# The last attention with V as the stationary operand, and its gate z kept by features

## The chip, the cores and the metric

The kernel runs on one core of one Trainium2 chip, as one program. The metric is the device time of an execution in microseconds. A profile is one further execution, taken by the hardware profiler. The engines have one instruction stream each and meet only at semaphores: TensorE (PE; its weight loads are listed as PEld), VectorE (DVE), ScalarE (ACT), GpSimd (POOL, all but unused here) and SyncE, which issues the loads.

## The reference, cut to what matters

Two transformer stacks follow each other on 256 tokens of width 1024. The change is in the last mixer of the second stack, a latent attention with 16 heads. Names are those of the kernel.

```python
xn = rmsnorm(x, g)                       # (256, 1024)
c, k_rope, z = xn @ w_in                 # latents 384 + 256, one rotary key, z (256, 1024)
q, kv = rms(c_q) @ w_qb, rms(c_kv) @ w_kvb   # 16 heads: 64 plain + 32 rotary features, V of 64
s = q_h @ k_h.T / sqrt(96)               # per head 256 x 256
p = softmax(s)                           # along the keys
o = (p @ v_h) * silu(z_h)                # per head 256 x 64
y = concat(o) @ w_out                    # (256, 1024)
```

After it come the residual, a norm, a gated projection and the final norm.

## The kernel before

All activations stay on the chip; weights stream through a ring of three slots, in units of at most 2048 columns. Each unit u is loaded to `raw`; ACT copies it to `high` (L582, a rounded value) and DVE subtracts to get `low` (L980); PE then multiplies three products per tile: high by high, high by low, low by high (`mm3`, L1565). The helper `behind(u)` on ACT and on DVE does this preparation for unit u + 3, so the place of each `behind` call in an engine's stream decides what stands in front of what. Nothing is scheduled by a planner: the order of each engine is the order of the code.

The projection z (PE L2067, `z_unit`) is made by tokens: the activations are stationary, 512 columns of weights move. Its result lies tokens by features in four banks; ACT takes it with a Silu scaled per token by `rcol` (L886). `rcol` is the inverse root of the norm, turned into a column by two PE transpositions (`root_columns(2)`, L1899) and a small DVE copy (`columns(2)`, L1329). Meanwhile DVE makes the norms of the latents: it reads the sums of squares that `latent_sums` (L2057) put into bank 2, takes a root (`newton`), scales five latents (L1505), and splits them for the next products.

The score products of heads 0 to 3 are put between the last units of the projections (j = 6 in the loop at L2101). The attention then runs over the 16 heads (PE L1955, ACT L789, DVE L1394). For each head PE transposes the exponentials `E2` in four pieces (`transposed`), ACT copies them to `PT2` (L797), and PE multiplies with the turned probabilities stationary and 65 columns of V moving, the 65th a column of ones, so that it gives the sum. DVE inverts the sum (L1401) and multiplies result, inverse and z (L1404). Scores of a pair of heads (two row tiles of 64, L2095 and L2097) are put in two pairs ahead. DVE takes the row maximum (L1392), ACT the exponential (L785). After the last head PE transposes the 16 pieces of the result back to features (`output_group`, L1980), ACT and DVE split them, and the output projection `feature_out` (L1863) begins.

The order of DVE around the start of the attention is: `behind` of the kvb units, the maxima of heads 0 to 3, `behind(first["mla_kvb"] + 3)` (L1527), and then `attention(False)`. ACT's is: exponentials of heads 0 and 1 at j = 6, the copies of j = 7, `behind` of the last kvb unit, and then the copy of the first turned head.

## Time and profile before

| | |
|---|---|
| median of 3 runs | 1094.41 us (1092.81 to 1095.01) |
| the profiled execution | 1093.67 us |
| its span, first to last instruction | 1091.9 us |
| granted clock, mean | 0.988 |
| PE / PEld busy | 95% / 88% of the span |
| DVE / ACT busy | 72% / 46% |
| DMA, mean | 192 GB/s |

PE's matmuls overlap in the profile, since each record also holds the time in the pipe: the step from one start to the next is what an instruction costs. A product of two plain float32 operands makes two records, a transposition one, and one of the three products of `mm3` one.

### The profile page before, as it was taken

Reading aid. Unit: us, or ns where it says so; the run is one execution under the profiler, and the core shown is the slowest. Engines: PE = TensorE matmul, PEld = TensorE weight load, DVE = VectorE, ACT = ScalarE, POOL = GpSimd, SP = SyncE. Lnnn points to the kernel's source line nnn. Section 1 sums busy time; section 2 is a strip of 40 time slices with the busy share of each in tenths; the row PEclk is TensorE's granted clock in tenths of the full one; section 3 lists DMA queues with packets and bytes.
Section 4 is the critical chain, followed back from the end, with each engine's and each line's share of the span. In section 5 each row is a group of like instructions: output and inputs, shape, how many; then the busy total and the mean of one; then the engine's idle time right before and its main releaser. Section 6 shows DMA issues by size and latency. Waiting matters only on the chain. (4 is left out here: it accounts for less than half of the span.)

```text
span 1091.9 us, 18245 instructions
## 1 busy us (share of the span) xinstructions
PE 1038.2 (95%) x7726; PEld 965.1 (88%) x7726; DVE 784.3 (72%) x1177; ACT 507.2 (46%) x700; POOL 0.7 (0%) x6
## 2 busy tenths in 40 slices
PE   4899999799999999998999999999999999999995
PEld 2689875699999999998999999999987998888984
DVE  3689759668788787887985656568736569786565
ACT  3623238554434334324443434445347556547462
POOL 0000000000000000000000000000000000000000
PEclk9899999999999999999999999999999999999998
DMA  9769541038898987566646666554754053445020
GB/s 368 269 210 337 185 173 39 2 117 292 307 317 291 312 289 237 196 222 228 242 165 221 201 234 219 176 175 149 234 183 139 7 192 127 162 166 198 1 78 38
DMA packets 116545, 210.15 MB, mean 192 GB/s; under 512 B 4251, under 2 KB 78193, under 8 KB 116465
## 3 DMA queue, kind: packets, MB, share of 16 engines
q1 hardware_dynamic: 115716, 206.81, 55.1%
q10 hardware_dynamic: 748, 2.18, 0.5%
q8 instruction: 61, 1.00, 0.4%
q14 instruction: 20, 0.16, 0.0%
HBM read 207.92 MB, written 1.05 MB: 191 GB/s over the span
## 5 line engine op out<-in xcount | busy, mean ns | idle before, releaser
L980 DVE TENSOR_TENSOR low<-raw,high 128x2048 fp32r<-128x2048 f32 (+2 forms) x147 | 328.1, 2234 | 159.8 <-ACT high L582 159.4
L582 ACT ACTIVATE high<-raw 128x2048 fp32r<-128x2048 f32 (+2 forms) x147 | 272.9, 1866 | 215.2 <-PE PS L1569 113.3
L1652 PE MATMUL PS<-hH,high 128*128 128x258 f32 x896 | 221.9, 284 | 4.5 <-ACT high L582 1.9
L1653 PE MATMUL PS<-hL,high 128*128 128x258 f32 x896 | 220.3, 283 | 0.0
L1652 PEld LDWEIGHTS PS<-hH,high 128*128 128x128 f32 x896 | 169.8, 189 | 6.4 <-issue 2.8
L1653 PEld LDWEIGHTS PS<-hL,high 128*128 128x128 f32 x896 | 168.7, 188 | 0.1
L1671 PE MATMUL PS<-hH,low 128*128 128x258 f32 x896 | 126.2, 283 | 0.3
L1671 PEld LDWEIGHTS PS<-hH,low 128*128 128x128 f32 x896 | 115.6, 189 | 1.4 <-DVE low L980 1.4
L1567 PE MATMUL PS<-gH,high 128*128 128x256 f32 x352 | 98.4, 280 | 0.0
L1568 PE MATMUL PS<-gL,high 128*128 128x256 f32 x352 | 98.4, 280 | 0.0
L1569 PE MATMUL PS<-gH,low 128*128 128x256 f32 x352 | 98.2, 279 | 0.0
L959 DVE SCALAR_TENSOR_TENSOR ada_acc<-ada_raw,cond,ada_acc 128x1024 f32<-128x1024 f32 x70 | 89.7, 1281 | 4.9 <-DMA ada_raw<-in_ada_w 2.7
L1567 PE MATMUL PS<-oH,high 128*128 128x256 f32 x256 | 73.9, 289 | 2.4 <-issue 1.8
L1568 PE MATMUL PS<-oL,high 128*128 128x256 f32 x256 | 73.3, 286 | 0.0
L1569 PE MATMUL PS<-oH,low 128*128 128x256 f32 x256 | 73.1, 286 | 0.0
L723 ACT ACTIVATE sil<-ta,shifts 128x256 f32<-128x256 f32 x44 | 20.0, 502 | 110.8 <-DVE ta L1224 110.8
L1567 PEld LDWEIGHTS PS<-gH,high 128*128 128x128 f32 x352 | 66.2, 188 | 0.2 <-DVE gL L1251 0.2
L1568 PEld LDWEIGHTS PS<-gL,high 128*128 128x128 f32 x352 | 66.0, 187 | 0.0
L1569 PEld LDWEIGHTS PS<-gH,low 128*128 128x128 f32 x352 | 66.0, 187 | 0.0
L1567 PEld LDWEIGHTS PS<-oH,high 128*128 128x128 f32 x256 | 49.5, 193 | 2.9 <-issue 1.8
L1567 PE MATMUL PS<-high,hH 128*128 128x512 f32 x128 | 51.3, 401 | 0.8 <-DVE low L980 0.8
L1568 PE MATMUL PS<-low,hH 128*128 128x512 f32 x128 | 50.4, 394 | 0.0
(315 smaller groups left out, 1935.3 us busy)
## 6 DMA issues: line engine op xcount, KB each, us to landing
raw<-in_ffn_w_in SPq DMA_DIRECT2D x44, 1024.0 KB, 6.2
ada_raw<-in_ada_w SPq DMA_DIRECT2D x82, 512.0 KB, 5.4
raw<-in_ffn_w_out SPq DMA_DIRECT2D x22, 1024.0 KB, 6.2
raw<-in_na_w_in SPq DMA_DIRECT2D x16, 1024.0 KB, 5.5
raw<-in_da_wqkv SPq DMA_DIRECT2D x12, 1024.0 KB, 8.7
raw<-in_sc_w_in SPq DMA_DIRECT2D x12, 1024.0 KB, 6.3
raw<-in_ple_w_gate SPq DMA_DIRECT2D x8, 1024.0 KB, 4.8
raw<-in_mla_w_in SPq DMA_DIRECT2D x7, 1024.0 KB, 5.3
```

Source lines behind the costliest of these rows:

```text
L582: nc.scalar.activation(high[s][:, 0:width(u)], raw[s][:, 0:width(u)], ACT.Copy).then_inc(high_ready, 1)
L723: ins = nc.scalar.activation(sil[:, c, :], ta[:, c, :], ACT.Silu, bias=shifts[:, c:c + 1])
L959: V_.scalar_tensor_tensor(acc[:, :], ada_raw[p % RING][:, :], cond[:, k, 0:1], acc[:, :], ALU.mult, ALU.add).then_inc(ada_used_dve, 1)
L980: V_.tensor_tensor(low[s][:, 0:w], raw[s][:, 0:w], high[s][:, 0:w].bitcast(F), ALU.subtract).then_inc(low_dve, 1)
L1567: MM(o, wH, xH, start=start, stop=False, skip_group_check=shared)
L1568: MM(o, wH, xL, start=False, stop=False, skip_group_check=shared)
L1569: return MM(o, wL, xH, start=False, stop=stop, skip_group_check=shared)
L1652: MM(PS[:, b + c, 0:SEQ + 2], high[s][w(j, c)], hH[:, j, 0:SEQ + 2], start=j == 0, stop=False)
L1653: MM(PS[:, b + c, 0:SEQ + 2], high[s][w(j, c)], hL[:, j, 0:SEQ + 2], start=False, stop=False)
L1671: last = MM(PS[:, b + c, 0:SEQ + 2], low[s][w(j, c)], hH[:, j, 0:SEQ + 2], start=False, stop=j == KC - 1)
```

## The change

It has four parts. First, the units of z are 256 columns wide over the whole depth, and PE makes z by features (`shared_features`: weights stationary, 256 tokens moving), one bank per unit; the banks are 3, 1, 2, 3. DVE scales each bank by the root, ACT takes the Silu in place on `zT` (the memory of X). The transposition of the root and its copy are gone. Secondly, the exponential of this attention also gives its row sums (`accum_out`), and DVE makes for each head two diagonal matrices with the inverses of the sums. PE turns E2 by a plain float32 product with such a diagonal instead of a transposition. Thirdly, V is stationary, 64 columns of it, and the 256 columns of the turned probabilities move; two heads lie side by side in partitions 0 to 63 and 64 to 127 of one bank. Fourthly, the results come out by features: DVE multiplies four heads at a time by z, ACT and DVE split them, and the 16 transpositions at the end are gone. The output projection waits for one quarter of them per unit.

```diff
-Z_BANK = ((3, 1), (2, 3))
+Z_BANK = (3, 1, 2, 3)
...
-    for c0 in (768, 768 + 512):
-        for half in range(2):
-            cols("mla", w["mla_w_in_2"][0], 4 * half, 4, c0, 512, 2)
+    for j in range(4):
+        cols("mla", w["mla_w_in_2"][0], 0, KC, 768 + 256 * j, 256, 1)
...
+        zT = X[:, :, :].rearrange(by_feature, n=SEQ)
+        diagonal = XN[:, 0, :].rearrange("p (i n) -> p i n", n=P)
...
-                                               bias=nmax[:, 2 * h + t:2 * h + t + 1])
+                                               bias=nmax[:, 2 * h + t:2 * h + t + 1],
+                                               accum_out=None if biased else esum[:, 2 * h + t:2 * h + t + 1])
...
-            act.wait_ge(root_column, 2)
-            for nb in range(2):
-                ua = first["mla_z"] + 2 * nb
...
-                for t in range(TT):
-                    act.wait_ge(blocks_done, blocks_before(ua + 1) + t + 1)
-                    nc.scalar.activation(Zg[:, t, 512 * nb:512 * nb + 512], bank(Z_BANK[nb][t]), ACT.Silu, scale=rcol[:, t:t + 1]).then_inc(vz_copied, 1)
...
+            for j in range(4):
+                behind(first["mla_z"] + j)
+                if j == 2:
                     for f0, f1 in ((0, 3), (3, 5)):
                         act.wait_ge(latent_staged, f1)
                         high_of(aH[:, f0:f1, :], latent[:, f0:f1, :])
+            for j in range(4):
+                act.wait_ge(z_scaled, j + 1)
+                nc.scalar.activation(zT[:, 2 * j:2 * j + 2, :], zT[:, 2 * j:2 * j + 2, :], ACT.Silu).then_inc(z_ready, 1)
...
-            attention(False)
...
+            def turned(h):
+                seen.next(made_a)
+                nc.scalar.activation(PT2[h % 2][:, :, :], bank(TURN_BANK[h % 2]).rearrange("p (k n) -> p k n", k=2), ACT.Copy).then_inc(probs_copied, 1)
+
+            def gated_high(q):
+                act.wait_ge(head_gated, 16 + q + 1)
+                high_of(oH[:, 2 * q:2 * q + 2, :], zT[:, 2 * q:2 * q + 2, :])
+
+            exps(2, False)
+            exps(3, False)
+            for p in range(8):
+                turned(2 * p)
+                turned(2 * p + 1)
+                if p + 2 < 8:
+                    exps(2 * p + 4, False)
+                    exps(2 * p + 5, False)
+                if p % 2 == 0 and p:
+                    gated_high(p // 2 - 1)
+            gated_high(3)
...
-            columns(2)
...
+            def z_bank(j):
+                v.wait_ge(blocks_done, block_end[first["mla_z"] + j])
+                V_.tensor_tensor(zT[:, 2 * j:2 * j + 2, :], bank(Z_BANK[j]).rearrange("p (k n) -> p k n", k=2), spread(rstd), ALU.mult).then_inc(z_scaled, 1)
+
             behind(first["mla_z"])
+            z_bank(0)
...
-            for u in range(first["mla_z"] + 1, first["mla_qb"]):
-                behind(u)
+            for j in range(1, 4):
+                behind(first["mla_z"] + j)
+                z_bank(j)
...
-            attention(False)
+
+            def diagonals(h):
+                seen.next(exp_ready)
+                link(V_.reciprocal(rsum[:, 2 * h:2 * h + 2], esum[:, 2 * h:2 * h + 2]))
+                for t in range(TT):
+                    ins = V_.tensor_scalar(diagonal[:, h % 4 * 2 + t, :], ident[:, :], rsum[:, 2 * h + t:2 * h + t + 1], None, ALU.mult)
+                ins.then_inc(diagonal_made, 1)
+
+            def gate_heads(q):
+                seen.next(value_made, 2)
+                z = zT[:, 2 * q:2 * q + 2, :]
+                V_.tensor_tensor(z, bank(VALUE_BANK[q % 2]).rearrange("p (k n) -> p k n", k=2), z, ALU.mult).then_inc(head_gated, 1)
+
+            def gated_low(q):
+                seen.next(split_high)
+                sl = slice(2 * q, 2 * q + 2)
+                V_.tensor_tensor(oL[:, sl, :], zT[:, sl, :], oH[:, sl, :].bitcast(F), ALU.subtract).then_inc(split_low, 1)
+
+            seen.n[exp_ready.name] = 32
+            v.wait_ge(z_ready, 4)
+            diagonals(0)
+            diagonals(1)
+            for p in range(8):
+                if p + 1 < 8:
+                    diagonals(2 * p + 2)
+                    diagonals(2 * p + 3)
+                if p + 2 < 8:
+                    scores(2 * p + 4, False)
+                    scores(2 * p + 5, False)
+                if p % 2:
+                    gate_heads(p // 2)
+                elif p:
+                    gated_low(p // 2 - 1)
+            gated_low(3)
...
-            z_unit(0, 0)
-            root_columns(2)
+            def z_unit(j):
+                shared_features(first["mla_z"] + j, Z_BANK[j])
+                owed(z_scaled, Z_BANK[j])
+
+            z_unit(0)
+            seen.n[root_ready.name] = 2
             latent_sums(2)
-            z_unit(0, 1)
-            z_unit(1, 0)
-            z_unit(1, 1)
+            for j in range(1, 4):
+                z_unit(j)
             seen.next(split_low, 2)
...
-            attention(mla_score, exp_ready)
-
-            outputs_around(None)
+            def turned_pair(p):
+                for h in (2 * p, 2 * p + 1):
+                    pe.wait_ge(diagonal_made, h + 1)
+                    b = TURN_BANK[h % 2]
+                    claim(b)
+                    for t in range(TT):
+                        for c in range(2):
+                            last = MM(PS[:, b, c * SEQ + t * P:c * SEQ + (t + 1) * P], E2[:, h % 4, t, c * P:(c + 1) * P],
+                                      diagonal[:, h % 4 * 2 + t, :], start=True, stop=True)
+                    last.then_inc(made_a, 1)
+                    owed(probs_copied, b)
+
+            turned_pair(0)
+            for p in range(8):
+                if p + 2 < 8:
+                    score_pair(2 * p + 4, mla_score, exp_ready)
+                seen.next(probs_copied, 2)
+                b = VALUE_BANK[p // 2 % 2]
+                if p % 2 == 0:
+                    claim(b)
+                for c in range(2):
+                    for e in range(2):
+                        last = MM(PS[64 * e:64 * e + 64, b, p % 2 * SEQ:(p % 2 + 1) * SEQ], V2[:, c, 2 * p + e, 0:64], PT2[e][:, c, :],
+                                  start=c == 0, stop=c == 1, tile_position=(0, 64 * e))
+                last.then_inc(value_made, 1)
+                if p % 2:
+                    owed(head_gated, b)
+                if p + 1 < 8:
+                    turned_pair(p + 1)
...
-            feature_out(first["mla_out"], (2, 0, 2, 0))
+            feature_out(first["mla_out"], (1, 1, 1, 1))
```

DVE at the start of the last attention: before, behind the subtraction for the last unit that is prepared there (`low`), come a maximum and the first head's inverse, which waits for a finished value product.

```order
L1392 TENSOR_REDUCE nmax<-PS 128x2 [waits score_made]
L1392 TENSOR_REDUCE nmax<-PS 128x2
L980 TENSOR_TENSOR low<-raw,high 128x2048 [waits high_ready]
L1392 TENSOR_REDUCE nmax<-PS 128x2 [waits score_made]
L1401 RECIPROCAL rsum<-PS 128x2 [waits value_made]
L1404 SCALAR_TENSOR_TENSOR XN<-PS,rsum,X 128x64 [waits dve_step]
L1404 SCALAR_TENSOR_TENSOR XN<-PS,rsum,X 128x64
```

```order
L1408 TENSOR_REDUCE nmax<-PS 128x2 [waits score_made]
L1408 TENSOR_REDUCE nmax<-PS 128x2
L996 TENSOR_TENSOR low<-raw,high 128x2048 [waits high_ready]
L1553 RECIPROCAL rsum<-esum 128x2 [waits exp_ready,z_ready]
L1555 TENSOR_SCALAR XN<-ident,rsum 128x128 [waits dve_step]
L1555 TENSOR_SCALAR XN<-ident,rsum 128x128
```

Now the diagonals (`XN<-ident,rsum`) stand behind the same subtraction, and what PE does first in the attention uses them.

PE in the last attention, a pair of heads in the middle: scores, then transpositions (L1578) and value products (L1975) head by head.

```order
L2095 MATMUL PS<-ml_kT,ml_qT 128x256 [waits exp_ready]
L2095 MATMUL PS<-ml_kT,ml_qT 128x256
L2097 MATMUL PS<-ml_krT,ml_qrT 128x256 x2
L2095 MATMUL PS<-ml_kT,ml_qT 128x256 x2
L2097 MATMUL PS<-ml_krT,ml_qrT 128x256 x2
L1578 MATMUL PS<-ident,E 128x128 [waits probs_copied,exp_ready]
L1578 MATMUL PS<-ident,E 128x128 x3
L1975 MATMUL PS<-V,PT 128x65 [waits head_gated,probs_copied]
L1975 MATMUL PS<-V,PT 128x65 x3
L1578 MATMUL PS<-ident,E 128x128 [waits probs_copied,exp_ready]
L1578 MATMUL PS<-ident,E 128x128 x3
```

```order
L2192 MATMUL PS<-XN,E 128x128 [waits diagonal_made,vz_copied,heads_copied,rope_part]
L2192 MATMUL PS<-XN,E 128x128 x3
L2192 MATMUL PS<-XN,E 128x128 [waits vz_copied,diagonal_made]
L2192 MATMUL PS<-XN,E 128x128 x3
L2141 MATMUL PS<-ml_kT,ml_qT 128x256 [waits exp_ready]
L2141 MATMUL PS<-ml_kT,ml_qT 128x256
L2143 MATMUL PS<-ml_krT,ml_qrT 128x256 x2
L2141 MATMUL PS<-ml_kT,ml_qT 128x256 x2
L2143 MATMUL PS<-ml_krT,ml_qrT 128x256 x2
L2207 MATMUL PS<-PT,V 64x256 [waits heads_copied,probs_copied]
L2207 MATMUL PS<-PT,V 64x256 x3
```

The second piece is the start of the attention in the changed kernel: both heads of a pair are turned together (L2192), then come the scores of a later pair, and four value products (L2207) do for two heads. The same kinds of rows repeat for each pair, without scores in the last two.

PE between the third and the fourth unit of z: the last products of the third unit and the first of the fourth, in the changed kernel.

```order
L1750 MATMUL PS<-hH,low 128x256 [waits low_dve]
L1750 MATMUL PS<-hH,low 128x256 x15
L1745 MATMUL PS<-hH,high 128x256 [waits z_scaled,high_ready]
L1746 MATMUL PS<-hL,high 128x256
```

Before, at the same place (third and fourth unit), with three rows that repeat for each tile:

```order
L1567 MATMUL PS<-high,hH 128x512
L1568 MATMUL PS<-low,hH 128x512
L1569 MATMUL PS<-high,hL 128x512
L1567 MATMUL PS<-high,hH 128x512 [waits low_dve]
L1568 MATMUL PS<-low,hH 128x512
```

The fourth unit waited only for its weights; now it takes bank 3 again, which DVE has to empty first (`z_scaled`).

## Rows read from the trace of the kernel before

**Rows 1.** Busy time by engine in 1000 to 1030 us (columns: stretch, engines, PEclk, DMA, GB/s).

```profile
1000.00:1030.00 30.00, 30.00 (x264) 27.21 (x263) 17.45 (x60) 17.54 (x41) 0.00 (x0) 1.00 0.10 36
```

**Rows 2.** Timeline of PE, last attention, one pair of heads (start, duration, instruction).

```profile
1010.21 0.70 PE L2095 MATMUL PS<-ml_kT,ml_qT 64*128 64x256 f32 x4
...
1012.14 0.66 PE L1578 MATMUL PS<-ident,E 128*128 128x128 f32 x4
1012.63 1.00 PE L1975 MATMUL PS<-V,PT 128*128 128x65 f32 x8
1013.47 0.61 PE L1578 MATMUL PS<-ident,E 128*128 128x128 f32 x4
...
1014.85 0.70 PE L2095 MATMUL PS<-ml_kT,ml_qT 64*128 64x256 f32 x4
```

**Rows 3.** Timeline of PE, first attention: a 128-column fp32 product beside a transposition.

```profile
200.50 1.16 PE L1858 MATMUL PS<-da_V,gates 128*128 128x128 f32 x8 [0.69 <-ACT gates L681]
201.49 0.60 PE L1578 MATMUL PS<-ident,gates 128*128 128x128 f32 x4
```

**Rows 4.** Timeline of PE, opening: four 32-column tiles in one PSUM bank.

```profile
19.73 0.62 PE L1753 MATMUL PS<-da_kT,cond 128*32 128x512 f32 x2 [0.41 <-DMA first_w<-in_ada_w]
19.74 0.62 PE L1753 MATMUL PS<-first_w,cond 128*32 128x512 f32 x2
20.18 0.60 PE L1753 MATMUL PS<-da_kT,cond 128*32 128x512 f32 x2
```

**Rows 5.** Timeline of PE, first and last waits of the last attention.

```profile
995.74 0.63 PE L1578 MATMUL PS<-ident,E 128*128 128x128 f32 x4 [1.48 <-ACT ml_kT L897]
...
1028.84 2.03 PE L1578 MATMUL PS<-ident,XN 128*128 128x128 f32 x16
1031.45 0.39 PE L1567 MATMUL PS<-oH,high 128*128 128x256 f32 x1 [0.59 <-DVE oL L1025]
```

**Rows 6.** Timeline of ACT, last attention; and one row of L665's view.

```profile
995.38 1.95 ACT L582 ACTIVATE high<-raw 128x2048 fp32r<-128x2048 f32 x1
...
1012.83 0.60 ACT L797 ACTIVATE PT<-PS 128x512 f32<-128x512 f32 x1 [2.03 <-PE PS L1578]
1013.32 0.83 ACT L785 ACTIVATE E<-PS,nmax 128x256 f32<-128x256 f32 x2
...
L665 ACT ACTIVATION_READ_ACCUMULATOR ada_raw<-PS,nmax x32: 188/199/223, 147.7 to 199.6; 128x1 f32 x32
```

**Rows 7.** Timeline of DVE, start of the last attention, and one smaller operation.

```profile
937.41 0.29 DVE L1012 TENSOR_SCALAR wide<-wide 128x256 f32<-128x256 f32 x1
...
997.36 2.29 DVE L980 TENSOR_TENSOR low<-raw,high 128x2048 fp32r<-128x2048 f32 x1 [2.62 <-ACT high L582]
999.57 0.68 DVE L1392 TENSOR_REDUCE nmax<-PS 128x2 f32<-128x512 f32 x1
1000.17 0.16 DVE L1401 RECIPROCAL rsum<-PS 128x2 f32<-128x2 f32 x1
```

**Rows 8.** Timeline of PE, the projection z.

```profile
944.52 0.38 PE L1578 MATMUL PS<-ident,rstd 128*128 128x128 f32 x2
946.36 2.40 PE L2063 MATMUL PS<-gates,ones 128*128 128x256 f32 x10 [1.46 <-DVE rcol L1332]
948.41 0.58 PE L1567 MATMUL PS<-high,hH 128*128 128x512 f32 x1
...
966.34 0.28 PE L1567 MATMUL PS<-ml_aH,high 128*128 128x256 f32 x1
```

**Rows 9.** Timeline of DVE, the projection z.

```profile
948.80 0.76 DVE L1494 TENSOR_SCALAR E<-PS 128x256 f32<-128x256 f32 x2 [2.58 <-PE PS L2063]
...
960.54 2.05 DVE L1505 SCALAR_TENSOR_TENSOR XN<-PS,cols,E 128x256 f32<-128x256 f32 x5
```

**Rows 10.** Timeline of PE after an idle time, and the clock just after.

```profile
207.63 3.42 PE L1578 MATMUL PS<-ident,XN 128*128 128x128 f32 x16 [3.70 <-DVE XN L1180]
...
208.00:210.00 2.00, 2.00 (x12) 1.82 (x11) 2.00 (x4) 1.30 (x2) 0.00 (x0) 0.51 0.00 0
```

More of the change, by code:

```diff
@@ L387, in build @@
         latent_staged = sem("latent_staged")
+        z_scaled = sem("z_scaled")
+        z_ready = sem("z_ready")
+        diagonal_made = sem("diagonal_made")
         rope_part = sem("rope_part")
@@ L879, in _ @@
             behind(u + 2)
-            act.wait_ge(root_column, 2)
-            for nb in range(2):
-                ua = first["mla_z"] + 2 * nb
-                behind(ua)
-                for t in range(TT):
-                    act.wait_ge(blocks_done, blocks_before(ua + 1) + t + 1)
-                    nc.scalar.activation(Zg[:, t, 512 * nb:512 * nb + 512], bank(Z_BANK[nb][t]), ACT.Silu, scale=rcol[:, t:t + 1]).then_inc(vz_copied, 1)
-                behind(ua + 1)
-                if nb == 0:
+            for j in range(4):
+                behind(first["mla_z"] + j)
+                if j == 2:
                     for f0, f1 in ((0, 3), (3, 5)):
@@ L905, in _ @@
                     exps(1, False)
-            attention(False)
-            for t in range(TT):
-                output_high(t, 0)
-            for t in range(TT):
-                output_high(t, 1)
+            def turned(h):
[15 more added lines that the diff above has]
+            gated_high(3)
             for u in range(first["mla_out"], first["mla_out"] + 2):
@@ L921, in _ @@
                 nc.scalar.activation(X[:, t, 512 * n:512 * n + 512], bank(2 * t + n), ACT.Copy).then_inc(x_ready, 1)
-            act.wait_ge(root_column, 3)
+            act.wait_ge(root_column, 2)
             for t in range(TT):
@@ L2065, in latent_sums @@
                 owed(c_sum_taken, b)
-            def z_unit(nb, half):
-                u = first["mla_z"] + 2 * nb + half
-                unit_ready(u)
-                for t in range(TT):
-                    b = Z_BANK[nb][t]
-                    if half == 0:
-                        claim(b)
-                    tokens(u, bank(b), hH, hL, 4 * half, 4, 0, t, half == 0, half == 1).then_inc(blocks_done, 1)
-                    if half == 1:
-                        owed(vz_copied, b)
-            z_unit(0, 0)
-            root_columns(2)
+            def z_unit(j):
[3 more added lines that the diff above has]
+            seen.n[root_ready.name] = 2
             latent_sums(2)
-            z_unit(0, 1)
-            z_unit(1, 0)
-            z_unit(1, 1)
+            for j in range(1, 4):
+                z_unit(j)
             seen.next(split_low, 2)
```

## The prediction

> **What bounds the kernel now.** I read the page first, then the busy time by stretch for the last attention, then the timelines of PE, ACT and DVE from the projection of z to the start of the output projection. In the middle of the last attention PE is busy for all of 30 us, while DVE and ACT work for 17.5 us each [rows 1]. So there only what PE does, or what makes it wait, counts. PE's first step waits 1.48 us for ACT's copies, and its last 16 transpositions are followed by a wait of 0.59 us for the splits [rows 5].
>
> **What a record costs.** Within a pair of heads the rows follow without a gap: from 1010.21 to 1012.14 the scores (1.93 us with the change to the next form), four transpositions 0.49, eight value records 0.84, transpositions and values of the second head 1.38, together 4.64 us per pair [rows 2]. The 65 columns of V cost 0.105 us a record, about what a transposition of 128 columns costs (0.12): here the load of the 128 stationary columns sets the pace. A full product of plain float32 with 256 moving columns costs (948.41 - 946.36)/10 = 0.205 us a record [rows 8].
>
> **The turning.** Four transpositions of one record become four products of two records, with the same shape as the first attention's value products: eight records of 128 columns took 0.99 us after a wait [rows 3], and eight value records 0.84 [rows 2]. I take 0.9 us a head, 1.8 a pair, where the transpositions took about 0.45: 16 x 0.45 = +7.2 us.
>
> **The values.** Before, 2 x 8 records at 0.105 = 1.7 us a pair. Now eight records of 256 moving columns. Alone in the array they would cost 8 x 0.205 = 1.64 us, side by side half. The trace has column tiles in the opening: four of 32 columns, in one bank, with different moving data. Two records of one pair of tiles start at 19.73, two of the other at 19.74, the next at 20.18 [rows 4], so four tiles run at once. The bounds are thus 0.82 and 1.64 us a pair. I take the lower, since the nearest row is of the same form, and 0.1 for the change of form: 0.96 us. The scores' first step after another form is about 0.1 us longer than the rest, and its record shows 0.70 against 0.61 and less [rows 2]. The Trainium skill, "TensorEngine Tiling", key properties, says that a change of tiling mode drains TensorE. That speaks against the change, which has three modes a pair instead of two. The rows put the drain at 0.1 us, so the sum has 8 x 0.1 = 0.8 us for it; a drain of the whole 0.3 us that a record stays in the pipe would make it 2.4.
>
> A pair in the middle is now 1.93 + 0.96 + 1.8 = 4.69 us, against 4.64. What the values give, the turning takes.
>
> **The ends of the attention.** From the first turning to the first output product it was 1031.45 - 995.74 = 35.7 us [rows 5]. Now: first turning 1.8, six pairs with scores 6 x 4.69 = 28.1, and two without. In these nothing lies between the turning and the values. An ACT copy of a turned head takes 0.60 us and starts 0.69 after the first of its four transpositions [rows 2, 6], that is about 0.25 after the last. So PE waits some 0.85 us before the last values, and before the values of the seventh pair 1.3, since ACT does the exponentials of heads 14 and 15 first. That is 1.3 + 0.96 + 1.8 + 0.85 + 0.96 = 5.9. Sum 35.8 us. The 16 transpositions and the wait behind them, 1031.45 - 1028.84 = 2.61 us [rows 5], are already out of it: the output projection needs one quarter of the results per unit, and the last quarter is split while three units run. This stage comes out even.
>
> ACT and DVE keep pace. ACT has per pair two copies at 0.5, four exponentials at about 0.4 (two took 0.83), each now with a read of the sum, 0.19 us long and about 0.1 in the stream [rows 6], and half a split: 3.2 of 4.69 us. DVE has two maxima at 0.6, two inverses at 0.2, four diagonals and one pass of 512 columns, 0.65. A diagonal of 128 columns lies between an inverse, 0.16, and a scaling of 256 columns, 0.29 [rows 7]: 0.2 each. DVE: 3.1 us.
>
> **The start of the attention is where it loses.** DVE makes the diagonals only behind `low` for the third unit of the output weights. In the trace ACT makes `high` of it from 995.38 [rows 6], behind the last copies; DVE starts `low` at 997.36 and is free at 999.57 [rows 7]. PE had been turning since 995.74 [rows 5]. Before, DVE's lateness had a cover: the first inverse was needed only at the first value product. Now it holds the first instruction of the attention, and behind that stand all scores and values. With the shifts of the parts before (1.0 earlier from z, below; 0.4 later for four reads of sums by ACT in front), `low` ends at 999.0. An inverse, two diagonals and the handoff are 0.7: PE starts at 999.7 instead of 995.74. That is +4.0 us, the whole gain of z included.
>
> **z.** The columns moved are the same, 96 x 512 = 192 x 256, twice the loads, hidden at this width; a unit is 5.6 to 5.7 us. The two transpositions and the wait for their copy go: the sums start at 944.6 instead of 946.36 [rows 8]. DVE's chain from the sums to the latents, 960.54 - 948.80 = 11.7 us [rows 9], thus begins at 947.0 and ends at 958.7. Then DVE scales the first bank of z, 0.7 us, and only at 959.5 is bank 3 free. PE has ended the third unit at 946.7 + 2 x 5.7 = 958.1 and waits 1.4 us. The fourth unit ends at 965.3 instead of 966.34 [rows 8]: -1.0 us. The Silus on ACT (four, behind a table load) end near 970, while the first copy of the next stage can wait until 974.8, when its bank is taken again; they are hidden. If they were not, the copies' 0.6 us would show.
>
> **The clock.** PE now stands still from about 993.4 to 999.7, 6.3 us. Once in the trace it stood for 3.70 us; the 16 transpositions behind it took 3.3 us instead of 2.0, and the granted clock in them was 0.51, the lower level of 1.2 GHz [rows 10]. With the first products at this level too I count 1.7 us. The same will happen here, and the work behind it is all on the path. The bounds are 0 and about 3 us.
>
> **Sum.** +4.0 (start) + 0.1 (attention with its end) + 1.7 (clock) = +5.8 us. The stage before is in the 4.0. From the profiled execution, 1093.67, that is 1099.5. This execution lies 0.74 below the median of the runs, so the forecast for the median is 1094.41 + 5.8 = 1100.2 us. Terms in the attention vary by their rates: 0.1 us a head on the turning is 1.6 us, the drain another 1.6.
>
> **Rivals.**
> 1. *The clock stays up* through the idle time. For it: the clock of rows 10 was read once only, and the moment at which it falls need not lie in this idle time. Against: there it fell after a shorter idle time. Time 1098.5.
> 2. *Two column tiles of 64 do not overlap* as four of 32 do. Then the values cost as much as before, 0.82 us more a pair, +6.6: 1106.8. For it: twice as many stationary columns to load for each tile. Against it: rows 4, and row tiles of 64 overlap too, since sixteen score records of 256 columns took 1.93 us and not 16 x 0.205 = 3.3. The Trainium skill, "TensorEngine Tiling", gotchas, says that row tiles cannot use one PSUM bank at once. The two heads share a bank, but as column tiles, as the four of rows 4 do; had the rule held for these, the time would be this one.
> 3. *Not slower*: a product with a diagonal costs PE one record, like a transposition, and not two. The turning would then stay at 0.45 us a head, -7.2, and the time 1100.2 - 7.2 = 1093.0, or with the clock up 1091.3. For it: the data moved are the same as in a transposition. Against: all plain products of float32 in the trace have two records. It comes within 0.2% of before once 8 of the 16 heads are so turned, (5.8 - 2.2)/0.45.
> 4. *The wait at the start is partly covered*: ACT's `high` for the unit comes earlier than in the trace by 2 us or more. For it: ACT has waits ahead of it. Against: they are for PE's products and for the maxima behind them, whose order stays. Time about 1097.
> 5. *A drift of the whole*: DVE or ACT limit a pair, because the exchange of PE, DVE (maximum), ACT (exponential), DVE (diagonal) is longer than I count. At 0.5 us a pair, 3 us more: 1103.
>
> **Chances.** The forecast with its own range of 1098.8 to 1102: 0.53. Rival 1: 0.13. Rival 2: 0.12. Rival 3: 0.05. Rival 4: 0.07. Rival 5: 0.10. The range of 1096.0 to 1105.5 leaves rivals 2 and 3 out, less than 2 in 10. A difference of 0.2%, 2.2 us, is about what a measurement of this kernel can tell from none. Faster by more needs rival 3 with the clock up: 0.03. Within it lie the rest of rival 3 and the lower part of 4: 0.09. Slower: 0.88.
>
> **What the profile will show.** PE's first turning starts near 999.7 in the old time, behind DVE's second diagonal, and the wait is put down to DVE; the granted clock there is near 0.5 for 3 to 4 us. The turning has two records per product, eight in 0.85 to 0.95 us. The value products' two tiles start in the same 0.02 us, and the eight records of a pair take 0.85 to 0.95; at 1.6 rival 2 holds. A pair in the middle takes 4.6 to 4.8 us. The fourth unit of z starts behind DVE's first scaling. The output projection starts without a wait for a split. I am wrong if the first turning starts before 997, or if pairs in the middle take under 4.3 or over 5 us.

## The result, and the profile of the changed kernel

| | before | changed |
|---|---|---|
| median, in one session on one chip | 1093.61 us (1091.77 to 1095.01) | 1101.00 us (1099.74 to 1101.21) |
| ratio, with its 95% interval | | 1.0066 (1.0053 to 1.0079) |
| span of the profiled execution | 1091.9 us | 1098.0 us |
| PE busy, share of the span | 95% | 95% |
| granted clock, mean | 0.988 | 0.986 |

The change costs 7.4 us; 5.8 were forecast. The two profiled executions are 6.1 us apart in span. Far ahead of the change they already differ by 1.3 us, the changed kernel being the earlier (PE's first instruction behind the wait of rows 10 starts at 206.30 instead of 207.63), so from here on I compare stretches between two places that both kernels have, and not absolute times. The common place is the end of the first unit of z: before, the first transposition of the root stood there, at 944.52 [rows 8]; now the sums of squares do. The first unit itself, which is changed too, takes 5.71 us instead of 5.54.

PE of the changed kernel from z to the start of the attention (start, duration, instruction, and in brackets the idle time and who ended it):

```profile
943.34 2.32 PE L2118 MATMUL PS<-gates,ones 128*128 128x256 f32 x10
...
958.26 0.35 PE L1745 MATMUL PS<-hH,high 128*128 128x256 f32 x1 [1.18 <-DVE X L1520]
...
985.15 0.70 PE L2141 MATMUL PS<-ml_kT,ml_qT 64*128 64x256 f32 x4
...
998.98 3.50 PE L2192 MATMUL PS<-XN,E 128*128 128x128 f32 x16 [7.08 <-DVE XN L1555]
1002.40 0.70 PE L2141 MATMUL PS<-ml_kT,ml_qT 64*128 64x256 f32 x4
```

The fourth unit of z waits 1.18 us for DVE to empty the bank; 1.4 were forecast. The first turning waits 7.08 us for a diagonal, where before it waited 1.48 us for a copy [rows 5], and its 16 records take 3.42 us to the next start. From the common place to the first turning it is 998.98 - 943.34 = 55.64 us; before it was 995.74 - 944.52 = 51.22. The start thus loses 4.4 us, the gain of z included.

DVE of the changed kernel in the same stretch (columns as for PE):

```profile
995.83 2.29 DVE L996 TENSOR_TENSOR low<-raw,high 128x2048 fp32r<-128x2048 f32 x1 [2.98 <-ACT high L586]
998.04 0.16 DVE L1553 RECIPROCAL rsum<-esum 128x2 f32<-128x2 f32 x1
998.24 0.48 DVE L1555 TENSOR_SCALAR XN<-ident,rsum 128x128 f32<-128x128 f32 x2
```

And ACT there, from the second unit of the output weights to the third:

```profile
986.23 1.91 ACT L586 ACTIVATE high<-raw 128x2048 fp32r<-128x2048 f32 x1 [0.37 <-DMA raw<-in_mla_w_out]
...
991.47 0.19 ACT L789 ACTIVATION_READ_ACCUMULATOR E<-PS,nmax 128x1 f32 x1
991.56 0.47 ACT L789 ACTIVATE E<-PS,nmax 128x256 f32<-128x256 f32 x1
...
993.86 1.94 ACT L586 ACTIVATE high<-raw 128x2048 fp32r<-128x2048 f32 x1
```

DVE could make the diagonals of heads 0 and 1 from the moment ACT had summed them, at 992.1 us for head 0 and 993.0 for head 1. It stands in front of `low` instead, idle for 2.98 us, because `low` needs the `high` that ACT ends at 995.8. That is the chain that the prediction named.

The granted clock there (columns: stretch, its length, busy time of PE, PEld, DVE, ACT, POOL with instructions, clock, DMA share, GB/s):

```profile
994.00:996.00 2.00, 0.00 (x0) 0.00 (x0) 0.17 (x1) 2.00 (x3) 0.00 (x0) 0.81 0.33 133
996.00:998.00 2.00, 0.00 (x0) 0.00 (x0) 2.00 (x1) 1.62 (x8) 0.00 (x0) 0.50 0.01 4
998.00:1000.00 2.00, 1.02 (x5) 1.06 (x6) 1.87 (x11) 0.00 (x0) 0.00 (x0) 0.50 0.37 39
1000.00:1002.00 2.00, 2.00 (x11) 2.00 (x11) 0.48 (x2) 0.60 (x1) 0.00 (x0) 0.50 1.00 408
1002.00:1004.00 2.00, 2.00 (x18) 1.75 (x19) 0.00 (x0) 0.60 (x1) 0.00 (x0) 0.98 0.19 78
```

PE stopped at 991.9, the clock fell to its lower level of 1.2 GHz in the window from 994 to 996, and came back at about 1002, after some 3 us of work. A pair in the middle, and the end of the attention, from the timeline of PE:

```profile
1004.33 1.08 PE L2207 MATMUL PS<-PT,V 128*64 128x256 f32 x8
1005.35 2.05 PE L2192 MATMUL PS<-XN,E 128*128 128x128 f32 x16
1007.33 0.70 PE L2141 MATMUL PS<-ml_kT,ml_qT 64*128 64x256 f32 x4
...
1029.96 2.05 PE L2192 MATMUL PS<-XN,E 128*128 128x128 f32 x16
1032.81 1.08 PE L2207 MATMUL PS<-PT,V 128*64 128x256 f32 x8 [0.80 <-ACT PT L910]
1033.83 2.05 PE L2192 MATMUL PS<-XN,E 128*128 128x128 f32 x16
1036.57 1.08 PE L2207 MATMUL PS<-PT,V 128*64 128x256 f32 x8 [0.69 <-ACT PT L910]
1037.58 0.39 PE L1622 MATMUL PS<-oH,high 128*128 128x256 f32 x1
```

From one start to the next the eight value records take 1.02 us (1005.35 - 1004.33), 16 turning records 1.98, the scores 1.92: 4.92 us a pair. The output projection follows without a wait, where before it had 0.59 us [rows 5].

**Where the 7.4 us are.** From the common place to the first output product: before 1031.45 - 944.52 = 86.93 us, now 1037.58 - 943.34 = 94.24, that is +7.3. Of it +4.4 is the start, +1.44 the lower clock in the first turning of this execution (3.42 instead of 1.98 us), and the rest, 7.31 - 4.42 - 1.44 = +1.45, the attention.

### The profile page after: what moved, and what is told of

The parts are those of the page before. It is cut to its first block, busy times and chain, and to the rows that moved or that the text cites. A ratio compares the mean times of both kernels' runs of the same rounds, so it can differ in the third digit from the quotient of the medians.

```text
span 1098.0 us, 18430 instructions
## 1 busy us (share of the span) xinstructions
PE 1039.8 (95%) x7804; PEld 966.7 (88%) x7804; DVE 788.0 (72%) x1184; ACT 509.5 (46%) x732; POOL 0.7 (0%) x6
## 3 DMA queue, kind: packets, MB, share of 16 engines
q8 instruction: 62, 1.02, 0.4%
## 4 chain that ended last, share of the span: by engine, by line
PE 77%; DVE 13%; ACT 4%; issue 2%; DMA 2%; SPq 1%; DVEq 0%; ACTq 0%
PE PS L1622 11%; PE PS L1623 11%; PE PS L1624 11%; PE PS L1707 8%; PE PS L1726 8%; PE PS L1708 7%; DVE low L996 3%; PE PS L1633 2%; PE PS L1745 2%; PE PS L1750 2%; PE PS L1746 2%; PE PS L1840 1%; DMA ada_raw<-in_ada_w 1%; PE PS L1841 1%; PE PS L1913 1%
## 5 line engine op out<-in xcount | busy, mean ns | idle before, releaser
L1623 PEld LDWEIGHTS PS<-oL,high 128*128 128x128 f32 x256 | 49.6, 194 | 0.0
L1624 PEld LDWEIGHTS PS<-oH,low 128*128 128x128 f32 x256 | 49.5, 194 | 0.0
```

What stands on the lines that cost most here:

```text
L1623: MM(o, wH, xL, start=False, stop=False, skip_group_check=shared)
L1624: return MM(o, wL, xH, start=False, stop=stop, skip_group_check=shared)
```

## The experiments

The measure for all but experiment 6 is the stretch from the first score product to the first output product: before 1031.45 - 987.51 = 43.94 us, changed kernel 1037.58 - 985.15 = 52.43 us. "Less" and "more" are against the changed kernel. Ratios are to the kernel before in the same session (medians of 1093.6 to 1093.9 us), with their 95% intervals; a time of one execution has none. The short names in the headings are those that the expectations use.

### 1. The diagonals of heads 0 and 1 ahead of `low` (e1)

```diff
-            behind(first["mla_kvb"] + 3)
             def diagonals(p):
...
             diagonals(0)
             diagonals(1)
+            behind(first["mla_kvb"] + 3)
```

> The changed kernel, with one step moved: DVE makes the diagonals of heads 0 and 1 before the subtraction for the third unit of the output weights, not behind it. Theory A (the first diagonals stood in that queue): the first turning starts behind ACT's copy of V, near 994.4 where it was 998.98; PE's idle time falls from 7.1 to about 2.5 us, the clock stays at its upper level, and the first turning takes 2.0 us, not 3.4. Sum -4.6 - 1.4 = -6.0 us against the changed kernel's 1101.0: about 1095. Rival B (the first turning is late for its exponentials or for ACT): it starts later than 997, and the time stays above 1099.

Measured: 1097.18 us, ratio 1.0034 (1.0019 to 1.0050). The stretch is 1038.29 - 990.23 = 48.06 us, 4.4 less. The timeline of PE at the first turning:

```profile
999.55 2.94 PE L2192 MATMUL PS<-XN,E 128*128 128x128 f32 x16 [2.58 <-DVE XN L1554]
1002.42 1.23 PE L2141 MATMUL PS<-ml_kT,ml_qT 64*128 64x256 f32 x4
```

The granted clock of this kernel just there (columns as in the windows above):

```profile
999.00:1000.00 1.00, 0.45 (x4) 0.48 (x5) 0.37 (x2) 1.00 (x2) 0.00 (x0) 1.00 0.98 406
1000.00:1000.50 0.50, 0.50 (x7) 0.50 (x6) 0.00 (x0) 0.50 (x1) 0.00 (x0) 0.95 0.12 41
1000.50:1001.00 0.50, 0.50 (x4) 0.50 (x3) 0.00 (x0) 0.50 (x1) 0.00 (x0) 0.50 0.00 0
```

The wait fell from 7.08 to 2.58 us, 4.5 us: the order of DVE is the cause of the late start. The clock did not stay up, as I had expected: PE began at the full clock, and after about 0.9 us of work the clock fell all the same, for about 3.4 us. What the first turning waits for now is ACT's copy of V, as the expectation has it. PE has a wait for it in its stream, and starts 0.22 us behind its end; the bracket names DVE, whose diagonals end at about the same time.

```profile
998.72 0.61 ACT L902 ACTIVATE V<-PS 128x512 f32<-128x512 f32 x1
```

### 2. The same kernel once more, for the clock (e11)

> The kernel of e1 once more, for a second reading of the clock. In e1 PE stood for 2.58 us, worked at the full clock for about 0.95 us, and then the clock fell to the lower level. Theory A: the moment is set by something that runs freely beside the program, so another execution can keep the clock: then the stretch from the first score product to the output projection is 48.06 - 1.4 = 46.6 us and the first 16 records take 2.0 us. Theory B: it is fixed by what the kernel does before and in the wait; then the same clock of 0.5 appears at the same place, some 3.8 us after PE stopped, and the stretch is 48.1 us again.

Measured: 1095.78 us (one execution). The stretch is 1033.47 - 985.37 = 48.10 us. PE at the first turning:

```profile
994.73 3.10 PE L2192 MATMUL PS<-XN,E 128*128 128x128 f32 x16 [2.62 <-DVE XN L1554]
997.76 1.23 PE L2141 MATMUL PS<-ml_kT,ml_qT 64*128 64x256 f32 x4
```

At this place theory A is not borne out: the clock fell again, 0.7 us after PE had begun (0.9 in experiment 1), though what lay ahead was 5 us apart between the two executions. But two executions do not rule it out, and elsewhere the same two traces speak for it. PE waits 1.72 us near 168 us, in instructions that the change does not touch. Behind this wait the clock fell in the execution of experiment 1 and stayed up in this one (columns as in the windows above; first experiment 1, then this execution):

```profile
171.63:173.63 2.00, 2.00 (x10) 2.00 (x11) 1.62 (x3) 1.10 (x4) 0.00 (x0) 0.50 0.60 206
169.24:171.24 2.00, 2.00 (x16) 1.30 (x14) 1.96 (x5) 1.83 (x6) 0.00 (x0) 1.00 0.63 216
```

Of the twelve profiled executions of this case four have the fall there (experiments 1, 4, 7 and 10). Behind the wait of 3.70 us that rows 10 show, all twelve have it, but it comes anywhere from 1.2 to 4.2 us after PE has stopped. So the instructions alone do not set the moment. Theory B is not shown either; that the clock fell twice at the start of this attention may be chance.

### 3. PE kept at work in the wait (e3)

40 products of no use, whose result nobody reads, ahead of PE's waits at the start of the attention:

```diff
+            claim(TURN_BANK[0])
+            for _ in range(40):
+                MM(PS[:, TURN_BANK[0], 0:SEQ], aH[:, 3, 0:P], aH[:, 3, :], start=True, stop=True)
             pe.wait_ge(heads_copied, seen.n[heads_copied.name + "/freed"])
```

> The changed kernel with 40 idle products of 256 columns on PE (results not used) in the idle time before the first turning. Theory A (the low clock is a cost of its own): they take about 4.8 us, the idle time left is about 2.3 us, the clock stays up, the first turning starts at the same place and takes 2.0 us, not 3.4: -1.4 us, about 1099.6. Rival B (the turning was slow for another reason, as a wait inside it): it still takes 3.4 us and the time is 1101.

Measured: 1099.46 us, ratio 1.0059 (1.0042 to 1.0075). The stretch is 1036.13 - 985.12 = 51.01 us, 1.42 less. PE, with the 40 products and the first turning:

```profile
991.71 4.96 PE L2184 MATMUL PS<-ml_aH 128*128 128x256 f32 x40
999.00 2.02 PE L2195 MATMUL PS<-XN,E 128*128 128x128 f32 x16 [2.34 <-DVE XN L1555]
```

The first turning starts when it did, its 16 records take 1.96 us to the next start, and the granted clock is 1.00 from 996 to 1002. So the lower clock cost 1.4 us, by itself. It is the profile that shows this: the interval of the ratio overlaps with that of the changed kernel (1.0053 to 1.0079). Here PE stood for 2.34 us and the clock held.

### 4. The order of the two column tiles (e4)

```diff
-                for c in range(2):
-                    for e in range(2):
+                for e in range(2):
+                    for c in range(2):
```

Each head's two products now follow each other, so that the tiles no longer alternate.

> The changed kernel with the four value products of a pair in another order: both of head 2p, then both of head 2p+1, where they alternated. Theory A (the two column tiles overlap only when neighbours in the stream use different tiles): each head's four records run one behind another at 0.205, with an overlap only in the middle, about 1.5 us for the eight records instead of 1.02, +0.5 us a pair, +4 us: about 1105. Rival B (PE overlaps them in any order, or the pace is set by something else): 1.02 us as before and 1101.

Measured: 1102.19 us, ratio 1.0079 (1.0064 to 1.0094); stretch 52.59 us. PE, the values of a pair and the start of the next turning:

```profile
1006.48 1.09 PE L2207 MATMUL PS<-PT,V 128*64 128x256 f32 x8
1007.50 2.05 PE L2192 MATMUL PS<-XN,E 128*128 128x128 f32 x16
```

1.02 us again. My theory was wrong, the rival right: in this kernel the order of the tiles is of no account.

### 5. Both heads in one column tile (e8)

The two heads go to the same 64 partitions and are added up there, so the results of the heads are not kept apart.

```diff
-                        last = MM(PS[64 * e:64 * e + 64, b, ...], ..., start=c == 0, stop=c == 1, tile_position=(0, 64 * e))
+                        last = MM(PS[0:64, b, ...], ..., start=c == 0 and e == 0, stop=c == 1 and e == 1, tile_position=(0, 0))
```

> The changed kernel with both heads' value products in the same column tile (the sum of two heads in partitions 0 to 63, so that the two heads are not kept apart). Theory A (side by side is what halves them): nothing can overlap, the eight records of a pair take 8 x 0.205 = 1.64 us or a little more, not 1.02, and a pair 5.55, not 4.92. Rival B (the products were not overlapped in the first place and cost 0.128 each by themselves): 1.02 us as before.

Measured: 1109.39 us (one execution). PE, the same place in a pair:

```profile
1018.67 1.94 PE L2207 MATMUL PS<-PT,V 128*64 128x256 f32 x8
1020.54 0.71 PE L2192 MATMUL PS<-XN,E 128*128 128x128 f32 x4
```

Eight records take 1.87 us in place of 1.02, 0.85 more a pair, and 8 x 0.85 = 6.8 of the 8.4 us that this kernel is slower than the changed one. Most of the rest is the lower clock, which in this execution lasted through the scores behind the first turning (3.06 us in place of 1.92, the turning 3.68 in place of 3.42). That the tiles overlap is thus shown, not only read from [rows 4]. The 1.87 us are 0.23 over 8 x 0.205 = 1.64, as the 1.02 are 0.2 over half of it.

### 6. z emptied ahead of the root of the latents (e5)

```diff
-            newton(four[3], four[2], four[0], four[1])
...
-            behind(first["mla_z"])
             z_bank(0)
+            newton(four[3], four[2], four[0], four[1])
+            behind(first["mla_z"])
```

> The changed kernel, with DVE's scaling of the first bank of z before the root of the latents, not behind it. Theory A (the fourth unit waits for bank 3 alone): PE's idle time of 1.18 us before the fourth unit is gone, and from the sums of squares (943.34 in the changed kernel's trace) to the first score product (985.15) it is 40.6 us, not 41.8. If the next units' weights become the wait, part of it comes back, up to 0.5 us. Rival B (something else holds the fourth unit): the idle time stays.

Measured: 1098.84 us (one execution). The wait ahead of the fourth unit is gone, and there is a new one behind it, in PE's timeline:

```profile
960.00 2.06 PE L1750 MATMUL PS<-hH,low 128*128 128x256 f32 x16
962.48 0.35 PE L1622 MATMUL PS<-ml_aH,high 128*128 128x256 f32 x1 [0.42 <-issue]
```

From the sums to the scores it is 983.72 - 942.60 = 41.12 us against 41.81: 0.7 of the 1.18 us stay.

### 7. The rows scaled on DVE, and plain transpositions again (e2)

Probabilities are divided by their sums in place, 2 x 256 columns a head on DVE, in place of the two diagonals; PE turns them by transposition.

```diff
-                    ins = V_.tensor_scalar(diagonal[:, h % 4 * 2 + t, :], ident[:, :], rsum[...], None, ALU.mult)
+                    ins = V_.tensor_scalar(E2[:, h % 4, t, :], E2[:, h % 4, t, :], rsum[...], None, ALU.mult)
...
-                            last = MM(PS[:, b, ...], E2[:, h % 4, t, c * P:(c + 1) * P], diagonal[...], start=True, stop=True)
+                    transposes(b, [(c * SEQ + t * P, P, E2[:, h % 4, t, c * P:(c + 1) * P]) for t in range(TT) for c in range(2)])
```

> The changed kernel, but DVE scales the two tiles of exponentials of a head in place by the inverse sums (2 x 256 columns) and PE turns them by transpositions, with no product with a diagonal. Theory A (the float32 product with two records is what makes a pair dear): turning a pair takes 1.0 us, not 1.98, a pair in the middle 3.95, not 4.92, and the eight pairs give 8 us; the first turning at the low clock costs 0.7 less as well: about 1092.5. Rival B (with PE shorter, the exchange of maximum, exponential, scaling and copy becomes the bound of a pair): a pair takes over 4.3 us, with PE waiting for ACT's copies or DVE's scaling, and the time is 1095 or more.

Measured: 1098.65 us, ratio 1.0045 (1.0029 to 1.0061); stretch 1037.37 - 987.12 = 50.25 us, 2.2 less. PE, first the turning of a pair in the middle, then the end of the attention:

```profile
1006.90 1.09 PE L1633 MATMUL PS<-ident,E 128*128 128x128 f32 x8
1007.92 0.70 PE L2141 MATMUL PS<-ml_kT,ml_qT 64*128 64x256 f32 x4
...
1031.55 1.33 PE L2203 MATMUL PS<-PT,V 128*64 128x256 f32 x8 [2.60 <-ACT PT L910]
1032.81 1.97 PE L1633 MATMUL PS<-ident,E 128*128 128x128 f32 x8
1035.46 1.97 PE L2203 MATMUL PS<-PT,V 128*64 128x256 f32 x8 [0.69 <-ACT PT L910]
```

DVE of this kernel in the middle of the attention:

```profile
1017.14 0.69 DVE L1566 TENSOR_TENSOR oL<-X,oH 128x512 fp32r<-128x512 f32 x1 [1.92 <-ACT oH L607]
1017.75 0.16 DVE L1553 RECIPROCAL rsum<-esum 128x2 f32<-128x2 f32 x1
```

The turning of a pair fell from 1.98 to 1.02 us. Eight times that is 7.7, and 5.5 of it went elsewhere: PE is now fast enough to be held up. DVE has `oL` ahead of the next inverse and stands 1.92 us for ACT's `oH`; PE then waits for the turned copy up to 2.60 us, and behind that wait the clock falls (0.50 from 1034 to 1038), so the last turning and the last values take nearly twice their time. The longer waits for turned copies are about 3 us of the 5.5, the lower clock at the end about 2.

### 8. The same, with the split of the results one pair later (e6)

```diff
                 if p % 2:
+                    if p > 1:
+                        gated_low(p // 2 - 1)
                     gate_heads(p // 2)
-                elif p:
-                    gated_low(p // 2 - 1)
```

> As the run with rows scaled and transposed, but DVE does the low part of a quarter of the results one pair later, behind ACT's high part and not waiting for it. In the run before, DVE waited 1.92 us for ACT there, and PE then waited 0.28, 0.71 and 2.60 us for turned heads. Theory A (that wait sets the pair): a pair takes 4.0 us throughout, PE's waits fall to about 0.8 and 0.7 us at the last two pairs, the clock stays up at the end, and from the first score product to the output projection it is 50.25 - 4 = about 46 us. Rival B (ACT's work itself is the bound): waits of 0.3 us or more a pair remain, and it is over 48 us.

Measured: 1094.98 us (one execution); stretch 1032.53 - 984.85 = 47.68 us, a further 2.6 less. PE at the start and near the end of the attention:

```profile
998.90 1.94 PE L1633 MATMUL PS<-ident,E 128*128 128x128 f32 x8 [7.31 <-DVE E L1555]
1000.77 1.23 PE L2141 MATMUL PS<-ml_kT,ml_qT 64*128 64x256 f32 x4
...
1028.67 1.08 PE L2203 MATMUL PS<-PT,V 128*64 128x256 f32 x8 [1.34 <-ACT PT L910]
```

The waits in the middle shrink to 0.3 us each, the longest is now 1.34, and the clock stays up at the end. It misses the 46 us that I had put down, for two reasons. The waits for turned copies still come to 2.65 us (0.29, 0.28, 1.34 and 0.74), where 1.5 were expected. And at the start the clock stayed low for 6.0 us of work: turning, scores and values took 1.87 + 3.71 + 1.23 = 6.81 us where at the full clock they take 3.96, so it cost 2.85 us here against 1.78 in experiment 7, behind the same wait of 7.31 us.

### 9. The start and z mended, the products with a diagonal kept (e10)

The edit of experiment 6, and the preparation of the third unit of the output weights (`behind(first["mla_out"] - 1)`) moved to the end of the attention on both engines, so that at the start neither DVE's `low` nor ACT's `high` stands in front:

```diff
-                behind(u)
+                if j < 7:
+                    behind(u)
...
+            behind(first["mla_out"] - 1)
             gated_high(3)
...
-            behind(first["mla_kvb"] + 3)
...
-            for u in range(first["mla_out"], first["mla_out"] + 2):
+            for u in range(first["mla_out"] - 1, first["mla_out"] + 2):
```

> The start and z are mended as in e7 (DVE's first scaling of z before the root of the latents, the unit before the output weights prepared at the end of the attention), but the probabilities are still divided by products with a diagonal, and the splits stand where the changed kernel has them. Theory A: PE's wait before the first turning is then 2.3 to 2.6 us, with the clock up, and the pairs take 4.92 us as in the changed kernel. From the first score product to the output projection: 52.43 - (7.08 - 2.4) - 1.44 for the clock = 46.3 us; with 0.7 from z the median is 1101.0 - 6.1 - 0.7 = about 1094.2, the same as before. What e7 has over this, 46.3 - 39.85 = 6.4 us, is then the price of the products with a diagonal, less the waits that e7 has in their place. Rival B: much of e7's gain in the attention comes from the later splits, which the products with a diagonal would also feel; then waits for PT appear inside the pairs here, or the stretch is over 47.5 us.

Measured: 1094.37 us against 1093.85, ratio 1.0007 (0.9995 to 1.0020): no difference from before. The stretch is 1031.66 - 985.58 = 46.08 us, as theory A has it (46.3), the pairs take 4.92 us, and no wait appears inside them. PE at the first turning:

```profile
994.52 2.02 PE L2193 MATMUL PS<-XN,E 128*128 128x128 f32 x16 [2.19 <-DVE XN L1556]
996.47 0.70 PE L2142 MATMUL PS<-ml_kT,ml_qT 64*128 64x256 f32 x4
```

### 10. All together: the edits of experiments 6 to 9 (e7)

> All together: rows scaled and transposed, the low part one pair later, z's first bank scaled first, and the preparation of the last weight unit before the output projection done by ACT and DVE at the end of the attention, not at its start. Theory A (each cost found stands by itself): from the first score product to the output projection 52.4 - 4.5 (start) - 8 (turning) = about 39.5 us, if the clock stays up, 1 us more if it falls; before it was 43.9. With the gains of z, 2.1 us against before, the kernel takes 1093.6 - 4.4 - 2.1 = 1087 us. Rival B (a stall moves to the output projection, whose third unit's weights are now late): PE waits in the projection, and the time is 1090 or more.

Measured: 1088.80 us against 1093.63, ratio 0.9957 (0.9944 to 0.9971): 0.4% faster than the kernel before, and 12 us faster than the changed one. The expectation had 1087 us, its rival 1090 or more. The stretch is 1026.37 - 986.52 = 39.85 us, against 39.5 expected. PE at the start, at its longest wait, and at the end:

```profile
995.60 1.06 PE L1634 MATMUL PS<-ident,E 128*128 128x128 f32 x8 [2.34 <-ACT V L902]
996.60 0.70 PE L2142 MATMUL PS<-ml_kT,ml_qT 64*128 64x256 f32 x4
...
1022.51 1.08 PE L2204 MATMUL PS<-PT,V 128*64 128x256 f32 x8 [1.34 <-ACT PT L911]
...
1026.37 0.39 PE L1623 MATMUL PS<-oH,high 128*128 128x256 f32 x1
```

At the start PE now waits for ACT's copy of V and no longer for DVE. The same holds for experiments 1 and 9: there too the first turning starts 0.2 us behind the end of this copy, whatever the bracket says. Against experiment 9 the transpositions are worth 46.08 - 39.85 = 6.2 us: the 7.7 of eight pairs, less 1.5 that the waits give back. This kernel also has the later split of experiment 8; the split was not tried with the products with a diagonal, but experiment 9 has no wait inside a pair that it could take away.

## Why the prediction was right, and where it was off

The difference is 7.4 us and 5.8 were forecast. That the median, 1101.0 us, lies within 0.8 us of the forecast of 1100.2 is in part luck: the kernel before took 0.8 us less when it was run beside the changed one (median 1093.61) than in the runs from which the forecast was counted (1094.41). By terms, the traces have +0.5 us at the start and +1.4 in the attention over the forecast, and -0.3 at the clock.

- **The start, +4.0 forecast, +4.4 measured.** Right in mechanism and size: experiment 1 moves that one `behind` and takes 4.5 us out of the wait. Two things lie over the forecast. ACT's `high` at 986.23 waits 0.37 us for a load, and with it all that follows on ACT and DVE comes 0.5 us later behind the first score product (986.23 - 985.15 = 1.08 us, before 988.11 - 987.51 = 0.60). And from the first inverse to the first turning it is 998.98 - 998.04 = 0.94 us, not 0.7. z gave 0.2 back.
- **z, -1.0 forecast.** From the common place to the first scores it is 41.81 us instead of 987.51 - 944.52 = 42.99: -1.2, and -1.0 with the 0.17 us that the first unit takes longer. The wait of 1.18 us for the bank was forecast as 1.4. Experiment 6 gets 0.7 of it back.
- **The clock, +1.7 forecast, +1.44 measured.** Experiment 3 takes out 1.42 with all else at its place. Rival 1 is out. But the 1.44 are of one execution. Experiments 4, 5 and 6 leave the start of the attention as it is in the changed kernel, and there turning and first scores took 5.41, 6.74 and 5.58 us, against 5.35 here and 3.90 at the full clock: the lower clock cost 1.4 to 2.8 us.
- **The values, 0.96 forecast, 1.02 measured.** The tiles overlap (experiment 5), so rival 2 is out. The forecast's own terms, 0.82 and 0.1, make 0.92 and not 0.96: by them the attention would have been put 0.3 us lower. At half of the 0.205 us of a record alone [rows 8] eight are 0.82 us, and 1.02 leaves 0.2 for the change of form, twice what the sum had for it and less than the 0.3 that a record stays in the pipe; experiment 5 has the same 0.2 in one tile. The Trainium skill, "TensorEngine Tiling (Array Packing)", key properties, says that a change of tiling mode drains TensorE; the trace does not contradict this, but no run here has a change of mode by itself, so what the 0.2 us are made of stays open.
- **The turning, 0.9 us a head forecast, 0.99 measured.** This is the term that was mis-sized, 16 x 0.09 = +1.4 us. The attention misses as much in all (+1.45 measured, +0.1 forecast), because the values (+0.5) and the waits near the end (-0.5) cancel. The row with this very shape said eight records in 0.99 us [rows 3]; I took 0.9, between it and the value products of [rows 2], whose 65 moving columns are fewer. The row with the same shape was the right one. Rival 3, one record per product, is out: 16 records a pair. The ranges put down for the profile were missed with it, if by little: 0.99 us for a head's turning (0.85 to 0.95), 1.02 for the values (0.85 to 0.95), 4.92 for a pair (4.6 to 4.8, and over 5 would have spoken against the forecast).
- **The end.** Forecast 1.3 and 0.85 us of waits, measured 0.80 and 0.69. The output projection did start without a wait.
- **Rivals 4 and 5.** The start was not covered, and no wait lies inside a pair. Rival 5's chain is real, but it shows only once a pair takes about 4 us (experiment 7).
- **My own theories behind the result** missed twice: I expected the clock to hold with the shorter wait of experiment 1, and the alternation of the tiles to matter (experiment 4). A third, on what sets the moment at which the clock falls, stays open (experiment 2).

In sum: the changed kernel's attention has no slack to give. It wins 0.7 us a pair on the values and loses 0.9 to 1.0 on the turning; what makes it slower by 7.4 us instead of about 1.5 is an order on DVE that before had a cover (4.5), and the clock behind it (1.4). Experiment 9 shows this from the other side: with the order mended and z's root later, the products with a diagonal come out even with before.

## What to carry to other kernels

When a change makes a helper engine's result the first need of the bound engine, look at what stands ahead of it in the helper's stream; what was hidden there is now on the path whole. Dividing on DVE, which had time to spare, and transposing was worth 6.2 us over a product that does both in one, since a plain float32 product is two records and a transposition one. And of several rows that could price an operation, take the one with its shape, not a mean with a cheaper neighbour. Last, one execution's clock is one draw: where the clock is a term, read it in several executions before giving it a price.

## What the hardware showed beyond the forecast

- In the last attention the clock fell behind every wait of PE of 2.58 us and more (7.1 to 7.5 us in the kernels with the late start, 2.62, 2.60 and 2.58 in experiments 2, 7 and 1) and behind none of 2.34 us and less (2.34 twice, 2.19, 1.48 and 1.34). With the two shorter ones of the first group it fell 0.7 and 0.9 us after PE had begun again at the start of the attention, and 0.7 us after at its end. But this order is no rule: near 168 us it fell behind 1.72 us in four of twelve executions, and did so in one and not in another execution of the same kernel (experiments 1 and 2). What decides stays open.
- Two column tiles of 64 with plain float32 overlap within one bank in either order, 1.02 us for eight records of 256 columns and a change of form, against 1.87 in one tile.
- The read of a row sum behind an exponential shows 0.19 us; from one exponential to the next it is 0.45 us (991.56 to 992.01), where two without it took 0.83 [rows 6].
- An idle wait for "issue" of 0.42 us appeared where a wait of 1.18 us had been taken away (experiment 6); it was there in the kernels of experiments 9 and 10 too. Its cause was not looked for.
